# Working LayerNorms, last output products and gate by column halves, and router logits straight into token rows, in a four-layer decoder trunk

## The chip, the cores and the metric

The kernel runs on one core of a Trainium2 chip (NeuronCore, with TensorE, VectorE, ScalarE, GpSimd and SyncE). The metric is the device time of one execution, in microseconds (us).

## The reference, cut to what matters

256 tokens of 1024 float32 columns pass four layers. A layer has a token mixer (layers 0 and 3 a short convolution, layer 1 retention, layer 2 a spatial gate), a LayerNorm, a mixture of 16 experts, a second LayerNorm and a gated embedding:

```python
x = _layer_norm(ALPHA * x + mix, ln_g[i, 0], ln_b[i, 0])
ffn = _moe(x, router_w, router_b, moe_w_gate[i], moe_w_up[i], moe_w_down[i])
x = _layer_norm(ALPHA * x + ffn, ln_g[i, 1], ln_b[i, 1])
emb = p[i] @ ple_w_proj[i]
gate = jax.nn.sigmoid(x @ ple_w_gate[i] + ple_b_gate[i])
x = x + gate * emb
```

The router inside `_moe` takes `sigmoid(hf @ router_w)` (1024 x 16), picks a group of four experts and two experts in it for every token, and weights their outputs.

## The kernel before, in words

The tokens are two tiles of 128 rows, `t` = 0 and 1, held in `x[:, t, :]` (token rows by 1024 columns). Weights of mixer, embedding projection and gate come as slots of 1 MB (128 x 2048), numbered through all layers; `starts[L]` gives the slot number of layer L's mixer, of its projection (one slot) and of its gate (four slots). Precision is kept by splitting each operand in a high and a low part: ScalarE copies a slot to `w_hi`, VectorE writes `w_lo` (one 128x2048 subtraction, L1319), and `product` issues three fp32r matmuls. `split_behind(used)` on ScalarE and VectorE splits all slots below `used + 4`. The activations are turned by TensorE (`transpose_tile`, L523, eight transposes, two PSUM banks or "quads" of four), then ScalarE saves `xT_hi` and VectorE `xT_lo` (`save_tile`); `turned_tile` makes TensorE wait for both quads' low parts. `k` = 3L+1, 3L+2 and 3L+3 number the turned versions of x in a layer.

`rows_slot` multiplies one slot for one tile: j = 0, 1 (128 rows of contraction each) by c = 0, 1 (512-column halves, each its own PSUM bank). The last slot of tile 0 gives `done`; for tile 1 `weights_used` is the signal.

A LayerNorm of one tile on VectorE is: `residual` (two L1345), `layer_norm` with two `bn_stats` (L1383), aggregation, then `moments`, a chain of small instructions each waiting for the one before, beside which the two halves of (x - mean) * g run (L1391), then one 128x1024 instruction times rstd plus b (L1396), which increments `x_tile_ready`. TensorE's transposes of a tile wait for that.

`route` computes the logits transposed: the stationary operand is `rw_pad` (high part of the router weights in columns 0 to 15, low part in 16 to 31, zeros behind), the moving operand is `xT`, 16 matmuls of 128 columns per tile (L779). ScalarE copies the result to `logitsT`, and two matmuls with `fold` (L798) turn it back to token rows and add the parts. In layers 1 and 2 the logits of tile 0 stand ahead of the embedding products of tile 0, in layers 0 and 3 behind the transposes of tile 1. Behind the logits TensorE has the embedding products of tile 1, and only then the two rank matmuls that the choice of experts waits for (L806, L807).

The experts run as eight pairs, 12 slots of 1 MB each, loaded by SyncE's queue as places come free (96 per layer, an order and places from `expert_places`). All engines go through the pairs in a written order. At the end `put_back` adds the last pair's rows into PSUM banks 0 to 3 (L844), c = 0 for both tiles and then c = 1 for both, and `ffn_done` counts. Then VectorE splits the first gate slot (`split_behind(n_gate - 3)`), reads the flag `crowded` and skips the code for crowded experts, and begins the second LayerNorm: tile 0, `save_tile`, three more gate slots split, tile 1, `save_tile`. TensorE does gate slots 0 to 2 of tile 0, transposes tile 1, slot 3, then tile 1. The gate itself is, per tile, two additions of `bgate` (L1766), one sigmoid over 1024 columns on ScalarE, and two 128x1024 instructions on VectorE (L1771, L1772). When tile 1 of a gate is done GpSimd loads the next layer's `p_in` (L481) to `emb`, and TensorE's `turn_p` (L544) waits for that. The last gate is followed by two stores of 128x1024.

## Time and profile before

| | us |
|---|---|
| median of 3 runs | 1782.9 (1781.86 to 1783.79) |
| the profiled execution, its own time | 1777.66 |
| its span, first to last instruction | 1775.9 |
| TensorE busy | 1644.1 (93%) |
| VectorE busy | 717.1 (40%) |
| ScalarE busy | 468.7 (26%) |

The profile holds one execution. Engines are PE (TensorE matmul), PEld (its weight loads), DVE (VectorE), ACT (ScalarE), POOL (GpSimd), SP (SyncE). L12 is line 12 of the kernel. A group in a timeline merges neighbours of one kind; in square brackets stands how long the engine was idle before it and what released it.

### The profile page before, as it was taken

To read this page: it belongs to the slowest core of one execution; us is meant where nothing else is said; L and a number is where in the kernel's file an instruction comes from. 1 tells how busy PE (TensorE), PEld (TensorE's weight loads), DVE (VectorE), ACT (ScalarE), POOL (GpSimd) and SP (SyncE) were. 2 spreads that over 40 slices of the span, in tenths; PEclk is the share of its full clock that TensorE was granted. 3 is DMA by queue.
4 is the path that set the end of the run, shared out by engine and by line. 5 is a ranking of instruction groups with operands and counts; after the bars stand their busy time and mean duration, and the time that the engine had idled before them with its cause. 6 is when DMAs were issued, how large, how long until landed. Compare 5 with 4: busy or idle time off the path is not lost.

```text
span 1775.9 us, 17856 instructions
## 1 busy us (share of the span) xinstructions
PE 1644.1 (93%) x7564; PEld 988.0 (56%) x7564; DVE 717.1 (40%) x1030; ACT 468.7 (26%) x545; POOL 16.8 (1%) x34
## 2 busy tenths in 40 slices
PE   6989999869999899998799999899996998999976
PEld 5874443258777743433588777544334877434325
DVE  3572111174757621111856656311116666111125
ACT  4531111044443211111344333211102452111111
POOL 0000000000000000000000000000000000000000
PEclk9989999989999999999899999899998998999998
DMA  7488999945443899999565447999994557999990
GB/s 282 177 347 319 423 421 421 420 190 205 163 173 133 331 386 421 422 420 421 190 261 197 148 151 282 367 420 421 421 421 200 207 228 303 376 422 421 420 387 24
DMA packets 77180, 547.99 MB, mean 309 GB/s; under 512 B 8608, under 2 KB 8608, under 8 KB 12320
## 3 DMA queue, kind: packets, MB, share of 16 engines
q1 hardware_dynamic: 73296, 530.95, 74.1%
q0 software_dynamic: 3792, 15.73, 2.4%
q8 instruction: 68, 1.11, 0.2%
q14 instruction: 24, 0.20, 0.0%
HBM read 545.60 MB, written 1.05 MB: 308 GB/s over the span
## 4 chain that ended last, share of the span: by engine, by line
PE 75%; DVE 12%; DMA 8%; ACT 3%; issue 2%; SPq 0%; ACTq 0%; DVEq 0%
PE psum L834 33%; PE psum L512 10%; PE psum L514 10%; PE psum L513 10%; DMA expert_work<-in_experts 6%; PE psum L826 4%; DVE w_lo L1319 4%; PE psum L844 3%; PE psum L523 3%; ACT w_hi L1028 2%; PE psum L779 1%; DVE x L1391 1%; DVE x L1396 1%; DVE x L1345 1%; DMA raw<-in_slots 1%
## 5 line engine op out<-in xcount | busy, mean ns | idle before, releaser
L1319 DVE TENSOR_TENSOR w_lo<-raw,w_hi 128x2048 fp32r<-128x2048 f32 x120 | 271.2, 2288 | 169.2 <-ACT w_hi L1028 168.2
L512 PE MATMUL psum<-w_hi,xT_hi 128*128 128x512 f32 x704 | 283.8, 403 | 17.5 <-DVE w_lo L1319 11.1
L513 PE MATMUL psum<-w_lo,xT_hi 128*128 128x512 f32 x704 | 279.0, 396 | 0.0
L514 PE MATMUL psum<-w_hi,xT_lo 128*128 128x512 f32 x704 | 278.8, 396 | 0.0
L1028 ACT ACTIVATE w_hi<-raw 128x2048 fp32r<-128x2048 f32 x120 | 224.9, 1909 | 97.0 <-PE psum L514 88.3
L834 PE MATMUL psum<-raw,xg 128*64 128x512 f32 x896 | 211.9, 599 | 3.8 <-DMA raw<-in_experts 3.8
L1028 ACT ACTIVATE work<-psum 128x512 f32<-128x512 f32 x156 | 90.9, 593 | 431.0 <-PE psum L514 207.0
L1319 DVE TENSOR_TENSOR work_r<-psum,work_r 128x512 fp32r<-128x512 f32 x84 | 56.7, 689 | 363.2 <-ACT work_r L1028 363.2
L512 PEld LDWEIGHTS psum<-w_hi,xT_hi 128*128 128x128 f32 x704 | 135.8, 193 | 51.7 <-DVE xT_lo L1319 9.3
L514 PEld LDWEIGHTS psum<-w_hi,xT_lo 128*128 128x128 f32 x704 | 135.1, 192 | 29.1
L513 PEld LDWEIGHTS psum<-w_lo,xT_hi 128*128 128x128 f32 x704 | 135.5, 193 | 27.8 <-issue 0.2
L1028 ACT ACTIVATE work_r<-psum 128x512 fp32r<-128x512 f32 x84 | 48.5, 598 | 331.5 <-PE psum L834 330.4
L834 PE MATMUL psum<-expert_work,xg 128*64 128x512 f32 x552 | 129.0, 598 | 0.0
L834 PEld LDWEIGHTS psum<-raw,xg 128*64 128x64 f32 x896 | 59.2, 136 | 114.0 <-issue 99.4
L834 PE MATMUL psum<-expert_high,xg 128*64 128x512 f32 x472 | 113.1, 600 | 1.7 <-DMA expert_high<-in_experts 1.6
L512 PE MATMUL psum<-w_hi,work_r 128*128 128x512 f32 x224 | 90.0, 402 | 11.6 <-DVE work_r L1319 10.6
L1028 ACT ACTIVATE xg<-psum 128x512 f32<-128x512 f32 x64 | 38.2, 597 | 213.3 <-PE psum L826 213.3
L523 PE MATMUL psum<-const,x 128*128 128x128 f32 x192 | 32.9, 328 | 66.2 <-DVE x L1396 60.9
L514 PE MATMUL psum<-w_hi,work_r 128*128 128x512 f32 x224 | 88.3, 394 | 0.0
L513 PE MATMUL psum<-w_lo,work_r 128*128 128x512 f32 x224 | 88.1, 393 | 0.0
L834 PE MATMUL psum<-expert_work,work 128*64 128x512 f32 x344 | 80.0, 595 | 3.4 <-DMA expert_work<-in_experts 3.4
L826 PEld LDWEIGHTS psum<-work_r 128*128 128x128 f32 x512 | 65.7, 190 | 27.2 <-issue 22.7
(151 smaller groups left out, 1470.6 us busy)
## 6 DMA issues: line engine op xcount, KB each, us to landing
raw<-in_experts SPq DMA_DIRECT2D x148, 1024.0 KB, 15.6
raw<-in_slots SPq DMA_DIRECT2D x120, 1024.0 KB, 4.9
expert_work<-in_experts SPq DMA_DIRECT2D x112, 1024.0 KB, 14.9
expert_high<-in_experts SPq DMA_DIRECT2D x96, 1024.0 KB, 15.7
expert_norm<-in_experts SPq DMA_DIRECT2D x20, 1024.0 KB, 13.8
ln_par<-in_ln_g POOLq DMA_DIRECT2D x8, 512.0 KB, 8.1
ln_par<-in_ln_b POOLq DMA_DIRECT2D x8, 512.0 KB, 12.0
expert_y<-in_experts SPq DMA_DIRECT2D x4, 1024.0 KB, 15.1
```

The costliest lines, as they stand in the source:

```text
L512: mm(out, lhs[0], rhs[0], start=start, stop=False)
L513: mm(out, lhs[0], rhs[1], start=False, stop=False)
L514: return mm(out, lhs[1], rhs[0], start=False, stop=stop)
L523: last = nc.tensor.transpose(psum[:, bank, i * P:(i + 1) * P], c, ident[:, :])
L779: last = mm(psum[:, 4, t * P:(t + 1) * P], rw_pad[:, j, :], xT[i][:, j, t * P:(t + 1) * P], start=i == 0 and j == 0, stop=i == 1 and j == ...
L826: last = mm(psum[:, bank, j * SEQ:(j + 1) * SEQ], x_split[a][:, t, chunk], pick[:, t, Q * SEQ:(Q + 1) * SEQ], start=t + a == 0, stop=t + a ...
L834: last = mm(psum[columns(e), bank, :], lhs(j, e), w[:, 2 * j + e, :], start=start and j == 0, stop=stop and j == 1)
L844: last = mm(psum[:, bank0 + 2 * t + c, :], where[:, t * P:(t + 1) * P], what[i][:, c * NB:(c + 1) * NB], start=start and i == 0, stop=stop ...
L1028: return nc.scalar.activation(dst, src, func)
L1319: return tt(lo, whole, hi.bitcast(F), ALU.subtract)
L1345: step(stt(xs, xs, ALPHA, psum[:, bank0 + 2 * t + c, :], ALU.mult, ALU.add))
L1391: step(stt(x[:, t, cols], x[:, t, cols], nmv[:, 0, 0:1], ln_par[:, 0, cols], ALU.subtract, ALU.mult))
```

## The change

- The residual and the statistics of a LayerNorm are done half by half (`add_rows`). The half c = 0 starts when its own columns are ready: `rows_slot` runs the last slot c by c and signals `half_done` when c = 0 is complete, and `put_half` does so for the experts' rows of tile 0.
- The last instruction of a LayerNorm is two of 512 columns, with `x_half_ready` and `x_tile_ready`; each quad of transposes waits for its own half.
- In the second LayerNorm the first gate slot's `w_lo` moves from ahead of tile 0's LayerNorm to between it and `save_tile`.
- The gate products wait quad by quad (`turned_quad`). The gate's additions, sigmoid, product and sum, and the final stores, are halves.
- The logits go straight into token rows: `xT` is stationary, the router weights (16 columns, `rw_split`) move; 24 matmuls per tile (high x high, high x low, low x high). `rw_pad`, `fold`, `logitsT`, the copy and L798 go. For tile 1 the 16 matmuls on `xT_hi` come ahead of the wait for `xT_lo`.
- The load into the place `xg` waits for `logits_done`, which comes in place of the transposed logits' signal.

```diff
-                    sp.wait_ge(logitsT_in_psum, L + 1)
+                    sp.wait_ge(logits_done, L + 1)
...
-                sp.wait_ge(x_tile_ready, 2 * (3 * DEPTH - 1) + t + 1)
-                sp.dma_start(out[0, t * P:(t + 1) * P, :], x[:, t, :]).then_inc(s_out, 16)
+                for c, ready in enumerate((x_half_ready, x_tile_ready)):
+                    cols = slice(c * NB, (c + 1) * NB)
+                    sp.wait_ge(ready, 2 * (3 * DEPTH - 1) + t + 1)
+                    sp.dma_start(out[0, t * P:(t + 1) * P, cols], x[:, t, cols]).then_inc(s_out, 16)
...
             def transpose_tile(k, t):
-                if k == 0:
-                    pe.wait_ge(s_x[t], 16)
-                else:
-                    pe.wait_ge(x_tile_ready, 2 * (k - 1) + t + 1)
                 for q in range(2):
+                    if k == 0:
+                        pe.wait_ge(s_x[t], 16)
+                    else:
+                        pe.wait_ge((x_half_ready, x_tile_ready)[q], 2 * (k - 1) + t + 1)
...
+                order = [(j, c) for j in range(2) for c in range(2)]
+                if s == count - 1:
+                    order = [(j, c) for c in range(2) for j in range(2)]
+                for j, c in order:
+                    last = product(psum[:, 2 * t + c, :], part(lhs, ALL, 2 * s + j, t),
+                                   part(w, ALL, 2 * j + c), s == 0 and j == 0, s == count - 1 and j == 1)
+                    if s == count - 1 and (j, c) == (1, 0) and done is not emb_in_psum:
+                        last.then_inc(half_done, 1)
...
+                def logits(t, q, a, b, start=False, stop=False):
+
+                    for j in range(4 * q, 4 * q + 4):
+                        last = mm(psum[:, 4, t * NE:(t + 1) * NE], xT[a][:, j, t * P:(t + 1) * P], rw_split[b][:, j, :],
+                                  start=start and j == 4 * q, stop=stop and j == 4 * q + 3)
                     return last
 
+                def logits_of_first_tile():
+                    for q in range(2):
+                        turned_quad(k, 0, q)
+                        logits(0, q, 0, 0, start=q == 0)
+                        logits(0, q, 0, 1)
+                        logits(0, q, 1, 0, stop=q == 1)
...
-                logits(1).then_inc(logitsT_in_psum, 1)
-                pe.wait_ge(logitsT_ready, L + 1)
-                for t in range(T):
-                    last = mm(psum[:, 6, t * NE:(t + 1) * NE], logitsT[:, t * P:(t + 1) * P], fold[:, :],
-                              start=True, stop=True)
+                for q in range(2):
+                    pe.wait_ge(xt_hi, 4 * k + 2 + q + 1)
+                    logits(1, q, 0, 0, start=q == 0)
+                    logits(1, q, 0, 1)
+                for q in range(2):
+                    turned_quad(k, 1, q)
+                    last = logits(1, q, 1, 0, stop=q == 1)
...
-                for t in range(T):
-                    put_back(place[1], y, t, 0, False, True)
+                put_back(place[1], y, 0, 0, False, True).then_inc(put_half, 1)
+                put_back(place[1], y, 1, 0, False, True)
...
-                turned_tile(3 * L + 2, 0)
                 for i in range(4):
+                    if i % 2 == 0:
+                        turned_quad(3 * L + 2, 0, i // 2)
...
-            def residual(t, bank0):
-
-                for c in range(2):
-                    xs = x[:, t, c * NB:(c + 1) * NB]
-                    step(stt(xs, xs, ALPHA, psum[:, bank0 + 2 * t + c, :], ALU.mult, ALU.add))
+            def add_rows(t, c):
+
+                xs = x[:, t, c * NB:(c + 1) * NB]
+                link(stt(xs, xs, ALPHA, psum[:, 2 * t + c, :], ALU.mult, ALU.add))
+                step(nc.vector.bn_stats(stats[:, t, c, :], xs))
...
-                stt(x[:, t, :], x[:, t, :], rstd, ln_par[:, 1, :], ALU.mult, ALU.add
-                    ).then_inc(x_tile_ready, 1)
+                for c, ready in enumerate((x_half_ready, x_tile_ready)):
+                    cols = slice(c * NB, (c + 1) * NB)
+                    stt(x[:, t, cols], x[:, t, cols], rstd, ln_par[:, 1, cols], ALU.mult, ALU.add).then_inc(ready, 1)
...
-                split_behind(n_gate - 3)
+                dve.wait_ge(put_half, L + 1)
+                add_rows(0, 0)
...
                 dve.wait_ge(ffn_done, T * L + 1)
-                residual(0, 0)
+                add_rows(0, 1)
                 layer_norm(0, 2 * L + 1)
+                split_behind(n_gate - 3)
                 save_tile(3 * L + 2, 0)
                 split_behind(starts[L][2])
                 dve.wait_ge(ffn_done, T * L + 2)
-                residual(1, 0)
+                for c in range(2):
+                    add_rows(1, c)
                 layer_norm(1, 2 * L + 1)
...
-                    dve.wait_ge(ple_sig, 2 * L + t + 1)
-                    link(tt(ple[:, t, :], ple[:, t, :], emb[:, t, :], ALU.mult))
-                    tt(x[:, t, :], x[:, t, :], ple[:, t, :], ALU.add).then_inc(x_tile_ready, 1)
+                    for c, ready in enumerate((x_half_ready, x_tile_ready)):
+                        cols = slice(c * NB, (c + 1) * NB)
+                        dve.wait_ge(ple_sig, 4 * L + 2 * t + c + 1)
+                        link(tt(ple[:, t, cols], ple[:, t, cols], emb[:, t, cols], ALU.mult))
+                        tt(x[:, t, cols], x[:, t, cols], ple[:, t, cols], ALU.add).then_inc(ready, 1)
```

## Rows read from the trace of the kernel before

**Rows 1.** Busy time by stretch: PE, PEld, DVE, ACT, POOL; granted clock, DMA share, GB/s.

```profile
146.00:358.00 212.00, 207.22 (x975) 80.55 (x972) 30.93 (x55) 28.09 (x46) 1.05 (x2) 1.00 1.00 412
358.00:408.00 50.00, 36.59 (x156) 29.24 (x156) 41.78 (x54) 18.60 (x16) 2.49 (x5) 0.86 0.45 173
632.00:636.00 4.00, 4.00 (x20) 1.29 (x18) 0.00 (x0) 0.00 (x0) 0.00 (x0) 1.00 0.73 260
1370.00:1372.00 2.00, 2.00 (x6) 1.53 (x5) 0.96 (x2) 0.28 (x1) 0.00 (x0) 0.50 0.96 315
```

**Rows 2.** Waits: who waited for whom, us in total, times, longest.

```profile
PE psum L523 <- DVE x L1396: 60.9, 12, 9.0
```

**Rows 3.** Timeline of VectorE behind layer 0's experts: start, us, instruction.

```profile
358.31 2.29 DVE L1319 TENSOR_TENSOR w_lo<-raw,w_hi 128x2048 fp32r<-128x2048 f32 x1 [1.11 <-ACT w_hi L1028]
360.52 1.28 DVE L1345 SCALAR_TENSOR_TENSOR x<-x,psum 128x512 f32<-128x512 f32 x2
...
366.13 1.28 DVE L1396 SCALAR_TENSOR_TENSOR x<-x,nrstd,ln_par 128x1024 f32<-128x1024 f32 x1
...
370.71 6.68 DVE L1319 TENSOR_TENSOR w_lo<-raw,w_hi 128x2048 fp32r<-128x2048 f32 x3
377.31 1.28 DVE L1345 SCALAR_TENSOR_TENSOR x<-x,psum 128x512 f32<-128x512 f32 x2
...
382.92 1.28 DVE L1396 SCALAR_TENSOR_TENSOR x<-x,nrstd,ln_par 128x1024 f32<-128x1024 f32 x1
```

**Rows 4.** Timeline of TensorE in the same stretch.

```profile
357.25 1.20 PE L844 MATMUL psum<-work_r 128*128 128x512 f32 x4 [0.29 <-DVE work_r L1319]
367.47 1.97 PE L523 MATMUL psum<-const,x 128*128 128x128 f32 x8 [9.02 <-DVE x L1396]
370.85 0.79 PE L512 MATMUL psum<-w_hi,xT_hi 128*128 128x512 f32 x1 [1.41 <-DVE xT_lo L1319]
384.26 1.10 PE L523 MATMUL psum<-const,x 128*128 128x128 f32 x8 [2.72 <-DVE x L1396]
```

**Rows 5.** Instructions on x by form: ns min/median/max, first and last start.

```profile
L1345 DVE SCALAR_TENSOR_TENSOR x<-x,psum x32: 677/680/687, 108.5 to 1745.1; 128x512 f32<-128x512 f32 x32
...
L1391 DVE SCALAR_TENSOR_TENSOR x<-x,nmv,ln_par x32: 739/743/746, 111.3 to 1748.1; 128x512 f32<-128x512 f32 x32
```

**Rows 6.** Timeline of TensorE in layer 0's routing.

```profile
124.58 1.97 PE L523 MATMUL psum<-const,x 128*128 128x128 f32 x8 [3.85 <-DVE x L1396]
126.20 1.95 PE L779 MATMUL psum<-xT_hi,rw_pad 128*128 128x128 f32 x8
...
131.36 1.91 PE L779 MATMUL psum<-xT_lo,rw_pad 128*128 128x128 f32 x8
...
134.61 0.77 PE L512 MATMUL psum<-w_hi,emb_r 128*128 128x512 f32 x1
```

**Rows 7.** Timeline of TensorE in layer 1's routing.

```profile
604.68 1.00 PE L779 MATMUL psum<-xT_hi,rw_pad 128*128 128x128 f32 x8
...
611.95 1.09 PE L523 MATMUL psum<-const,x 128*128 128x128 f32 x8 [2.55 <-DVE x L1396]
614.61 1.97 PE L779 MATMUL psum<-xT_hi,rw_pad 128*128 128x128 f32 x8 [1.57 <-DVE xT_lo L1319]
...
619.63 0.77 PE L512 MATMUL psum<-w_hi,emb_r 128*128 128x512 f32 x1
```

**Rows 8.** Timeline of ScalarE in the same stretch.

```profile
610.40 1.06 ACT L1028 ACTIVATE work_r<-x 128x1024 fp32r<-128x1024 f32 x1
```

**Rows 9.** Timeline of VectorE at the last gate.

```profile
1767.75 1.42 DVE L1766 TENSOR_TENSOR work<-psum,bgate 128x512 f32<-128x512 f32 x2 [5.72 <-PE psum L514]
...
1771.60 1.22 DVE L1772 TENSOR_TENSOR x<-x,work 128x1024 f32<-128x1024 f32 x1
```

**Rows 10.** The chain that ended last, layer 0's gate: start, us, what.

```profile
406.56 3.13 DMA emb<-in_p
```

**Rows 11.** Timeline of ScalarE behind layer 0's experts.

```profile
356.37 3.70 ACT L1028 ACTIVATE w_hi<-raw 128x2048 fp32r<-128x2048 f32 x2
```

More of the change, by code:

```diff
@@ L198, in build @@
         conv_w = conv_w.rearrange("p (i w j) -> p i w j", i=2, w=3)
-        rw_pad = sb("rw_pad", KD, P, dt=FR)
-        fold = sb("fold", NE)
+        rw_split = [sb(f"rw_{part}", KD, NE, dt=FR)[:, :, :] for part in ("hi", "lo")]
         stats = sb("stats", T, 6, 6)
@@ L286, in build @@
         xt_in_psum, xt_ready = sem("xt_in_psum"), sem("xt_ready")
-        x_tile_ready = sem("x_tile_ready")
+        x_half_ready, x_tile_ready, half_done = sem("x_half_ready"), sem("x_tile_ready"), sem("half_done")
+        put_half = sem("put_half")
         mix_done, mix_read = sem("mix_done"), sem("mix_read")
@@ L595, in rows_slot @@
                 w = slot(n + s)
-                for j in range(2):
-                    for c in range(2):
-                        last = product(psum[:, 2 * t + c, :], part(lhs, ALL, 2 * s + j, t),
-                                       part(w, ALL, 2 * j + c), s == 0 and j == 0, s == count - 1 and j == 1)
+                order = [(j, c) for j in range(2) for c in range(2)]
[6 more added lines that the diff above has]
+                        last.then_inc(half_done, 1)
                 if t == 1:
@@ L1104, in conv_mixer @@
                     act.wait_ge(s_const, 16)
-                    act.wait_ge(rw_zeroed, 1)
-                    copy(rw_pad[:, :, 0:NE], rw[:, :, :]).then_inc(rw_hi_ready, 1)
+                    copy(rw_split[0], rw[:, :, :]).then_inc(rw_hi_ready, 1)
                 for k in range(4):
@@ L1200, in route @@
             def route(L):
-                act.wait_ge(logitsT_in_psum, L + 1)
-                copy(logitsT, psum[:, 4, 0:SEQ]).then_inc(logitsT_ready, 1)
                 act.wait_ge(logits_done, L + 1)
-                copy(score[:, :, :], psum[:, 6, 0:T * NE].rearrange("p (t e) -> p t e", t=T), ACT.Sigmoid
+                copy(score[:, :, :], psum[:, 4, 0:T * NE].rearrange("p (t e) -> p t e", t=T), ACT.Sigmoid
                      ).then_inc(score_ready, 1)
@@ L1292, in _ @@
                             save_tile(3 * L + 3, 0)
[L1293 to L1294 removed]
+                    for c in range(2):
+                        cols = slice(c * NB, (c + 1) * NB)
+                        act.wait_ge(ple_arg, 4 * L + 2 * t + c + 1)
+                        copy(ple[:, t, cols], ple[:, t, cols], ACT.Sigmoid).then_inc(ple_sig, 1)
         @block.vector
@@ L1378, in layer_norm @@
             def layer_norm(t, k, banks_read=None):
-                ready = steps[0]
-                for c in range(2):
-                    dve.wait_ge(dve_step, ready - 1 + c)
-                    step(nc.vector.bn_stats(stats[:, t, c, :], x[:, t, c * NB:(c + 1) * NB]))
                 dve.wait_ge(dve_step, steps[0])
@@ L1720, in experts @@
                                     xs = x[:, t, c * NB:(c + 1) * NB]
-                                    last = stt(xs, psum[:, 4 + 2 * t + c, :], 1 / ALPHA, xs, ALU.mult, ALU.add)
+                                    scale = 1 / ALPHA if t + c else 1.0
+                                    last = stt(xs, psum[:, 4 + 2 * t + c, :], scale, xs, ALU.mult, ALU.add)
                             last.then_inc(o["vector"], 1)
                     dve.wait_ge(o["vector"], len(OVER["vector"]) * PAIRS * ROUNDS)
+                    nc.vector.bn_stats(stats[:, 0, 0, :], x[:, 0, 0:NB]).then_inc(o["vector"], 1)
+                    dve.wait_ge(o["vector"], len(OVER["vector"]) * PAIRS * ROUNDS + 1)
             save_tile(0, 0)
@@ L1727, in _ @@
                 (conv_mixer, retention_mixer, sgu_mixer)[L % 3](L)
-                end = starts[L][1]
+                end, n_gate = starts[L][1:3]
                 split_behind(end - 4)
+                dve.wait_ge(half_done, 4 * L + 1)
+                add_rows(0, 0)
                 wait_rows(dve, L, 0, mix_done, L + 1, end)
-                residual(0, 0)
+                add_rows(0, 1)
                 layer_norm(0, 2 * L)
@@ L1748, in _ @@
                 dve.wait_ge(ffn_done, T * L + 1)
-                residual(0, 0)
+                add_rows(0, 1)
                 layer_norm(0, 2 * L + 1)
+                split_behind(n_gate - 3)
                 save_tile(3 * L + 2, 0)
@@ L1753, in _ @@
                 dve.wait_ge(ffn_done, T * L + 2)
-                residual(1, 0)
+                for c in range(2):
+                    add_rows(1, c)
                 layer_norm(1, 2 * L + 1)
                 save_tile(3 * L + 2, 1)
-                n_gate = starts[L][2]
                 dve.wait_ge(bg_loaded, 16 * (L + 1))
```

46 lines of the change are left out of this document (19 added, 27 removed).

## The prediction

> **What bounds the kernel now.** I read the page first: a span of 1775.9 us (the table above). Then the busy time by stretch [rows 1]: during layer 0's experts PE is busy 207.22 of 212 us at the full clock with DMA at 1.00, so two resources are full and nothing the change touches is. From the end of the experts through the gate PE works 36.59 of 50 us while DVE works 41.78: here LayerNorm on DVE sets the pace. The waits [rows 2] say the same: transposes waited 60.9 us, 12 times, for the last instruction of a LayerNorm. So I followed DVE and PE in order of time behind the experts [rows 3, 4], in routing [rows 6 to 8], and at the end [rows 9].
>
> The reader is to see in [rows 3, 4]: the last expert rows are issued at 357.25 (TensorE's L844); DVE then splits a gate slot (358.31 to 360.60), and only then starts the residual (360.52); 5.61 us later (366.13) starts the last instruction, 1.28 us. PE has been idle 9.02 us when it transposes, and 1.41 us more before its first product at 370.85. Tile 1 repeats it: three slots split from 370.71, residual at 377.31, transposes at 384.26 after 2.72 us idle. Behind these PE is full again, so what tile 1's transposes gain passes on.
>
> **Second LayerNorm and gate, four times.** (a) w_lo moved: 2.29 us leave the path ahead of tile 0's LayerNorm. (b) Tile 0's half c = 0 is added behind the last y rows (357.2) and costs 0.68 + 0.04 + 0.68 = 1.40 us [rows 5], the statistics taking as long, so to 358.6, while TensorE ends c = 1. The second half then starts at 358.6 and gives its statistics at 360.05; before, residual and statistics took 2.5 us from 360.52. Gain (a) and (b): 2.97 us; the last instruction starts at 363.16. (c) As two halves it costs 2 x 0.743 less 0.07 overlap = 1.41 for 1.28 us, but quad 0 can be transposed 0.55 us earlier than before the split. That helps little for tile 0: the moved w_lo now stands between, 364.55 to 366.8, and xT_lo of quad 0 follows at 367.45. The first product starts at 367.5 for 370.85, 3.3 us earlier. (d) The three w_lo start at 368.0 and end at 374.6; tile 1's four half steps, each waiting for the one before, take 2.75 for 2.51 us, the last instruction starts at 380.5, x_half is ready at 381.25 and x_tile at 381.9. Quad 1 is turned by 382.5, when slot 3 begins; before, 385.1. **2.6 us per layer, 10.4 in all.** What PE gained in tile 0 is lost again in a longer wait for tile 1. SP's queue has no part: the gate slots were issued from 335.77 on, the first row of the queue behind the experts, and landed before their splits.
>
> **The gate's halves** gain nothing between layers: PE goes on with tile 1's slots. They cost: product and sum as four linked halves take about 2.76 for 2.49 us, the projection's input is loaded after that, and TensorE waits for its landing [rows 10]: +0.25, three times, **+0.8**. Behind the last gate nothing covers them: from 1767.75 to 1772.82 [rows 9] 5.07 us; now half 0 is added while half 1 is multiplied by TensorE, then come 0.73 of addition and 2.8 of halves: 3.55. The last store is half as large. **-1.8.**
>
> **Routing.** The new logits are 24 matmuls per tile of 16 moving columns. Their nearest price is the old one, which has the same 128x128 fp32r loads: from 126.20 to 131.36, 24 matmuls, 0.215 us each at 1.2 GHz [rows 6], about 0.105 at 2.4 GHz (the eight at 604.68, [rows 7]). I take these, since the stationary load was already what spaced 128 moving columns.
> Layers 0 and 3: the halves bring transposes 1.1 us forward (0.55 by the statistics of half 0, 0.55 by the split; DVE is held by a w_lo until 116.9). From there 48 matmuls instead of 32 (+3.4 us), no copy and no fold (133.07 to 134.61, -1.5). Together **+0.8 each**.
> Layers 1 and 2: tile 0's logits stand in the shadow of tile 1's LayerNorm (8 more, 0.85 us warm; PE idled 2.55 there). For tile 1 the LayerNorm ends 1.0 us earlier, but ScalarE, whose split of x at 610.40 moves behind the later embedding copy to 611.25, frees xT_hi only at 612.85, when 24 matmuls start: 612.9 + 5.1 = 618.0 for 619.63 [rows 7, 8]. **-1.6 each.** The load into `xg` then waits for a signal that comes at the same time as its old one.
> Routing in all: 1.6 - 3.2 = **-1.6**. Is it passed through the experts? DMA fills up only behind their first products, so an earlier start moves the whole stretch as long as DMA has idle time to give; in the tightest, layer 1, DMA had 27% of 4 us free at 632 [rows 1], 1.1 us, and smaller gaps after it. I count it all.
>
> **Unseen terms.** The `crowded` test on DVE (read a flag, skip code) was under the 2.29 us w_lo, which left no gap [rows 3], so it costs at most 2.2 us; now only 0.68 us of statistics cover it. Between 0 and 1.5 us is exposed, four times (0 to 6 us). ScalarE does the same between two copies of 1.85 us that stand back to back [rows 11], so I stay low: +0.3 each, **+1.2**. The clock: behind tile 1's transposes it was at 0.50 in layer 2 (1370 to 1372, six matmuls started in 2 us, [rows 1]) but at 1.00 in layer 0, after PE had stood idle. The new idle, 378.2 to 381.3 and between quads, is some 0.7 us longer. A cold stretch of 3.5 us costs half of itself, 1.8 us; four layers, two of them cold already: 0 to +3.8, I take **+1.0**.
>
> The Trainium skill (Runtime: NRT & Kernel Launch, Instruction fetch mechanics) says that a taken branch out of the two fetched pages waits for a DMA fetch, which speaks against moving cover off this skip; the row only shows that the wait, if any, is under 2.2 us. At that bound the sum would be 4.8 us worse.
>
> **Sum**: -10.4 + 0.8 - 1.8 - 1.6 + 1.2 + 1.0 = -10.8 us. The profiled execution's own 1777.66 (1.76 outside the span) would become 1766.9; the median of runs lies 5.2 above it, so I predict 1782.9 - 10.8 = **1772.1 us**.
>
> **Rivals.**
> 1. Skip exposed: DVE stands 1.5 us before tile 0's second half in each layer. For: nothing else covers it. Against: ScalarE's gapless row. +4.8: 1777. Chance 0.11.
> 2. Clock lost: longer gaps and 2.5 us of light 16-column matmuls let the clock fall also in layers 0 and 1's gate and before the embedding products of layers 1 and 2; 2.8 more in the gate, 1.2 x 2 in routing: 1777. For: it fell in layers 2 and 3. Against: in layer 1 the transposes at 611.95 were still warm behind 2.55 us of idle [rows 7]. Chance 0.12.
> 3. Both, or one with the experts giving nothing back: 1780 to 1783, no measurable change. Chance 0.05.
> 4. Cheap loads: not the load but the 128 moving columns bound L779, and 16 columns are spaced by half, 0.107 at 1.2 GHz. Layers 0 and 3 gain 5.1 each, layers 1 and 2 (held by xT_lo until 614.2) 2.9 each: 1756. Against: with 128 columns the spacing is twice the array time, so the load binds. Chance 0.06. The Trainium skill (TensorE: Matmul & The Clock Gate, LDWEIGHTS) puts a load at columns / 1.2 ns, 107 ns for 128; no row shows that for this type at 1.2 GHz.
> 5. Slower: a 16-column matmul costs two passes, as a plain f32 one (L798, two instructions each, 0.43 us) does. Then routing pays 48 x 0.215 in layers 0 and 3 (10.3 each) and 5.1 + 2 in layers 1 and 2: +35 in all, 1807. It decides from about 0.29 us per matmul: 144 of them on the path (2 x 48 + 2 x 24) x 0.075 = 10.8. Against: operands stay fp32r, one instruction each in L779. Chance 0.03.
> The forecast itself: 0.63.
>
> **How the numbers follow.** Faster by over 0.2% (3.6 us, about what can be told from no change) is the forecast, 1, 2 and 4: 0.92; same 0.05; slower 0.03. The range takes in 1 and 2 with a margin for a skip and clock in between, to 1778, and below a warm routing in layers 1 and 2 (3 us) and no exposed terms (2.2), with 1 more: 1765. Outside lie 3, 4, 5 and small tails, under 0.2.
>
> **What the new profile would show.** Right: from the last expert row to the residual's second half about 1.3 us; transposes at 6.7 us behind it for 10.2; idle before tile 1's transposes above 3 us; first gate product 3.3 us earlier; logits 0.21 us apart at 1.2 GHz; score about 0.8 later against the mixer's end in layers 0 and 3, 1.5 earlier in 1 and 2. Wrong: a gap on DVE behind `put_half` with nothing running; cold matmuls in slot 3 of layers 0 and 1; logits at another spacing; a layer whose experts end no earlier though they start earlier.

## The result: faster, by 17 to 21 us where 10.8 were predicted

Changed kernel: 1761.15 us (median of 4 runs, 1759.79 to 1763.59), beside 1782.38 for the kernel before (4 runs). The ratio is 0.9884, 95% interval 0.9859 to 0.9909, so 16 to 25 us less. Two more sets of runs of the same kernel, with the experiments, gave 0.9905 (0.9881 to 0.9929) and 0.9890 (0.9871 to 0.9909). The predicted 1772.1 us is a ratio of 0.9939: right in direction, too small, and 1765, the lower end of the range, is above the measured time. The profiled spans are 1775.9 and 1758.2 us, 17.7 less, with a mean granted clock of 0.965 and 0.970.

The page of the changed kernel:

```profile
span 1758.2 us, 17988 instructions
...
PE 1650.8 (94%) x7612; PEld 993.7 (57%) x7612; DVE 721.3 (41%) x1060; ACT 468.7 (27%) x549; POOL 16.8 (1%) x34
```

Busy time by stretch, columns as in [rows 1]:

```profile
146.00:358.00 212.00, 206.48 (x971) 79.88 (x968) 31.19 (x56) 27.24 (x45) 1.05 (x2) 1.00 1.00 411
358.00:408.00 50.00, 39.80 (x172) 31.57 (x172) 43.01 (x61) 20.52 (x20) 3.36 (x6) 0.86 0.49 186
846.00:863.00 17.00, 11.70 (x45) 9.12 (x44) 16.58 (x24) 4.79 (x4) 0.00 (x0) 0.80 0.08 32
863.00:875.00 12.00, 12.00 (x52) 10.10 (x51) 7.86 (x10) 5.84 (x6) 1.81 (x3) 0.89 0.53 177
```

PE's share is 94% for 93, DVE's 41% for 40. The experts' stretch is as full as before. In the 50 us from 358 PE now gets 39.80 us done for 36.59, since the stretch holds more products. DVE is as busy as it was: it is still what sets the pace here, only with less ahead of it.

VectorE behind layer 0's experts, as [rows 3]:

```profile
357.66 0.68 DVE L1356 SCALAR_TENSOR_TENSOR x<-x,psum 128x512 f32<-128x512 f32 x1
358.37 0.69 DVE L1357 BATCH_NORM_STATS2 stats<-x 128x6 f32<-128x512 f32 x1
359.52 0.69 DVE L1356 SCALAR_TENSOR_TENSOR x<-x,psum 128x512 f32<-128x512 f32 x1 [0.45 <-PE psum L855]
...
364.07 1.41 DVE L1406 SCALAR_TENSOR_TENSOR x<-x,nrstd,ln_par 128x512 f32<-128x512 f32 x2
365.40 2.29 DVE L1331 TENSOR_TENSOR w_lo<-raw,w_hi 128x2048 fp32r<-128x2048 f32 x1
...
368.80 6.68 DVE L1331 TENSOR_TENSOR w_lo<-raw,w_hi 128x2048 fp32r<-128x2048 f32 x3
375.40 0.68 DVE L1356 SCALAR_TENSOR_TENSOR x<-x,psum 128x512 f32<-128x512 f32 x1
...
381.26 1.41 DVE L1406 SCALAR_TENSOR_TENSOR x<-x,nrstd,ln_par 128x512 f32<-128x512 f32 x2
383.39 1.35 DVE L1331 TENSOR_TENSOR xT_lo<-psum,xT_hi 128x512 fp32r<-128x512 f32 x2 [0.72 <-ACT xT_hi L1041]
```

TensorE there, as [rows 4]:

```profile
357.80 1.20 PE L855 MATMUL psum<-work_r 128*128 128x512 f32 x4 [0.29 <-DVE work_r L1331]
364.87 1.97 PE L522 MATMUL psum<-const,x 128*128 128x128 f32 x8 [5.87 <-DVE x L1406]
368.34 0.79 PE L511 MATMUL psum<-w_hi,xT_hi 128*128 128x512 f32 x1 [1.50 <-DVE xT_lo L1331]
...
382.07 1.32 PE L522 MATMUL psum<-const,x 128*128 128x128 f32 x8 [2.50 <-DVE x L1406]
383.14 0.47 PE L511 MATMUL psum<-w_hi,xT_hi 128*128 128x512 f32 x1
```

Counted from the last expert row (357.25 before, 357.80 now), tile 0's transposes come after 7.07 us for 10.22, its first product after 10.5 for 13.6, tile 1's transposes after 24.27 for 27.01. The first half of the residual starts before the last row is issued; the gap ahead of the second half, where the flag is read and code skipped, is 0.45 us here (0.18, 0.52 and 0.17 in layers 1 to 3).

Layer 1's routing, TensorE, as [rows 7]:

```profile
602.51 0.51 PE L786 MATMUL psum<-rw_hi,xT_hi 128*128 128x16 f32 x4
602.87 0.59 PE L786 MATMUL psum<-rw_lo,xT_hi 128*128 128x16 f32 x4
...
604.65 0.59 PE L786 MATMUL psum<-rw_hi,xT_lo 128*128 128x16 f32 x4
...
609.35 1.24 PE L522 MATMUL psum<-const,x 128*128 128x128 f32 x8
612.15 0.61 PE L786 MATMUL psum<-rw_hi,xT_hi 128*128 128x16 f32 x4 [1.57 <-ACT xT_hi L1041]
...
614.69 1.85 PE L786 MATMUL psum<-rw_hi,xT_lo 128*128 128x16 f32 x8
616.40 0.77 PE L511 MATMUL psum<-w_hi,emb_r 128*128 128x512 f32 x1
```

Granted clock behind tile 0's logits there, 1.00 in the 2 us before:

```profile
606.00:610.00 4.00, 4.00 (x15) 3.12 (x14) 2.50 (x9) 0.42 (x1) 0.00 (x0) 0.57 1.01 428
```

Logits with 16 moving columns start 0.111 us apart at the full clock (16 from 602.87 to 604.65) and 0.214 at half (eight from 614.69 to 616.40). Layer 2 came out differently:

```profile
1105.97 1.32 PE L522 MATMUL psum<-const,x 128*128 128x128 f32 x8
1108.52 0.61 PE L786 MATMUL psum<-rw_hi,xT_hi 128*128 128x16 f32 x4 [1.23 <-ACT xT_hi L1041]
...
1110.33 1.04 PE L786 MATMUL psum<-rw_hi,xT_lo 128*128 128x16 f32 x8
```

All 24 logits of tile 1 run at the full clock here, and the next product starts 5.25 us after the transposes began; with the old logits it was 7.69 there.

The last gate, VectorE, as [rows 9]:

```profile
1752.48 0.69 DVE L1784 TENSOR_TENSOR work<-psum,bgate 128x512 f32<-128x512 f32 x1 [0.67 <-PE psum L513]
...
1755.13 0.69 DVE L1791 TENSOR_TENSOR x<-x,work 128x512 f32<-128x512 f32 x1
```

From the bias addition behind the last product (now one half, before two) to the end of the span it is now 5.7 us, for 8.15.

Where the 17.7 us of the two profiled executions lie, by layer 0 to 3 (us, time after less time before):

| stretch | 0 | 1 | 2 | 3 | sum | predicted |
|---|---|---|---|---|---|---|
| up to the first gather of the experts | -0.4 | -1.8 | -3.9 | +1.6 | -4.6 | -1.6 |
| experts | +1.0 | +1.0 | 0.0 | -1.4 | +0.6 | 0 |
| last expert row to tile 1's transposes | -2.7 | -3.0 | -2.7 | -3.0 | -11.4 | -10.8 |
| from there to the next layer's first embedding transposes, or the end | 0.0 | +1.4 | -0.1 | -3.7 | -2.3 | +1.6 |

(Predicted, third row: four times 3.0 earlier, less 1.2 for the skip, is -10.8. Fourth row: of the 3.0 only 2.6 were to pass slot 3 of tile 0, four times +0.4, and +1.6 + 0.8 + 1.0 - 1.8 = +1.6. The first row counts from the embedding transposes, in layer 0 from the start of the span; what stands there ahead of the mixer's end took 0.3 us longer.)

### The profile page after: what moved, and what is told of

Its sections match the earlier page's. It is cut to its first block, busy times and chain, and to the rows that moved or that the text cites. A ratio compares the mean times of both kernels' runs of the same rounds, so it can differ in the third digit from the quotient of the medians.

```text
span 1758.2 us, 17988 instructions
## 1 busy us (share of the span) xinstructions
PE 1650.8 (94%) x7612; PEld 993.7 (57%) x7612; DVE 721.3 (41%) x1060; ACT 468.7 (27%) x549; POOL 16.8 (1%) x34
## 4 chain that ended last, share of the span: by engine, by line
PE 76%; DVE 12%; DMA 8%; ACT 2%; issue 1%; SPq 0%; DVEq 0%; ACTq 0%
PE psum L845 34%; PE psum L511 10%; PE psum L512 10%; PE psum L513 10%; DMA expert_work<-in_experts 6%; DVE w_lo L1331 4%; PE psum L837 4%; PE psum L855 3%; PE psum L522 2%; PE psum L786 2%; ACT w_hi L1041 1%; DVE work_r L1331 1%; DMA raw<-in_slots 1%; DVE x L1399 1%; DVE stats L1357 1%
## 5 line engine op out<-in xcount | busy, mean ns | idle before, releaser
L1663 DVE TENSOR_REDUCE cg<-psum 128x1 f32<-128x256 f32 x32 | 13.6, 425 | 160.2 <-PE psum L899 160.2
## 6 DMA issues: line engine op xcount, KB each, us to landing
ln_par<-in_ln_b POOLq DMA_DIRECT2D x8, 512.0 KB, 11.4
```

## The experiments

Each set is timed beside the kernel before on its own chip. Their medians of before were 1780.62 (21 runs: `again`, `wlo_only`, `wlo_back`, `route_only`), 1783.14 (15 runs: `warm`, `route_back`, `gate_full`, `before_again`) and 1781.32 (9 runs: the last four), so ratios are compared, not times.

| run | median (n), us | ratio to before, 95% |
|---|---|---|
| again | 1763.67 (6) | 0.9905 (0.9881 to 0.9929) |
| wlo_only | 1770.57 (6) | 0.9940 (0.9920 to 0.9960) |
| wlo_back | 1773.77 (10) | 0.9961 (0.9945 to 0.9978) |
| route_only | 1779.61 (12) | 0.9996 (0.9979 to 1.0013) |
| route_back | 1764.22 (5) | 0.9898 (0.9876 to 0.9921) |
| gate_full | 1763.56 (6) | 0.9892 (0.9866 to 0.9917) |
| warm | 1773.08 (10) | 0.9954 (0.9937 to 0.9970) |
| before_again | 1779.65 (1) | single run |
| third | 1764.51 (5) | 0.9890 (0.9871 to 0.9909) |
| warm_fit | 1763.70 (5) | 0.9897 (0.9882 to 0.9913) |
| lo_late | 1762.52 (5) | 0.9888 (0.9873 to 0.9904) |
| late_t1 | 1752.09 (5) | 0.9830 (0.9814 to 0.9847) |

**again**, the changed kernel as it is.

> The changed kernel once more. Chain theory (the time comes out of LayerNorm's and the gate's chain as worked out before, and the clock only adds chance): the gain against before varies between executions with where the clock falls, 17 to 21 us in the median, and the stretches ruled by VectorE (last expert row to tile 1's transposes) repeat to 0.5 us at 24.0 us, while those in which TensorE ran cold differ by 1 to 3 us between this profile and the first one. Rival (all of the excess is a fixed mis-sizing): every stretch repeats within 0.3 us.

Measured -17 us for -21; the two intervals overlap, and the gain stays above 10.8 (12.6 at the least). As the chain theory had it, the stretches from the last expert row to tile 1's transposes repeat within 0.02 us, and those in which TensorE's clock fell differ by up to 1.8.

**wlo_only**: the kernel before with the w_lo alone moved.

```diff
-                split_behind(n_gate - 3)
...
                 layer_norm(0, 2 * L + 1)
+                split_behind(starts[L][2] - 3)
                 save_tile(3 * L + 2, 0)
```

> The kernel before with one edit: the first gate slot's w_lo moves behind tile 0's second LayerNorm. Chain theory: VectorE had 1.84 + 0.16 us idle waiting for xT_hi, which the moved 2.29 us now fill, so tile 1's transposes come 2.0 us earlier behind the last expert row in each layer, 8 us in all: ratio 0.9955. Clock theory (most of the gain of the whole change is TensorE running at the full clock in stretches where it was cold): under 4 us from the chain, and the rest follows the cold time in the profile, up or down.

10 us less: the move alone does half or more of what the change does. Tile 1's transposes come 24.53 to 24.55 us after the last row in every layer, 2.47 sooner. VectorE of this kernel:

```profile
359.32 1.28 DVE L1345 SCALAR_TENSOR_TENSOR x<-x,psum 128x512 f32<-128x512 f32 x2 [0.83 <-PE psum L844]
...
366.14 2.28 DVE L1319 TENSOR_TENSOR w_lo<-raw,w_hi 128x2048 fp32r<-128x2048 f32 x1
```

Where the w_lo stood there is a gap of 0.83 us and then the residual. Before, the 2.29 us were not all: VectorE had first waited 1.11 us for ScalarE's w_hi [rows 3]. My step (a) priced the move at the instruction's duration. The times of step (b) left the wait out all the same, so the sum of both did not suffer.

**wlo_back**: the changed kernel with the w_lo put back ahead of tile 0's first half.

```diff
+                split_behind(n_gate - 3)
                 dve.wait_ge(put_half, L + 1)
...
                 layer_norm(0, 2 * L + 1)
-                split_behind(n_gate - 3)
```

> The changed kernel with the first gate slot's w_lo put back ahead of tile 0's LayerNorm (ahead of the early half). Chain theory: 2.0 us slower than the changed kernel per layer, 8 us, so about 12 to 13 us faster than before. If the clock gives most of the gain, the loss is under 4 us.

Half to two thirds of the gain is gone. Its VectorE:

```profile
358.79 2.29 DVE L1331 TENSOR_TENSOR w_lo<-raw,w_hi 128x2048 fp32r<-128x2048 f32 x1 [1.11 <-ACT w_hi L1041]
361.00 0.68 DVE L1356 SCALAR_TENSOR_TENSOR x<-x,psum 128x512 f32<-128x512 f32 x1
...
362.86 0.69 DVE L1356 SCALAR_TENSOR_TENSOR x<-x,psum 128x512 f32<-128x512 f32 x1 [0.45 <-issue]
```

The wait of 1.11 us is back, and tile 1's transposes are 26.7 to 27.1 us behind the last row, as in the kernel before: with the w_lo ahead of them the halves bring 0.3 us at most in this LayerNorm. There is a gap of 0.45 us which here no other engine ends ("issue"; 0.17, 0.52 and 0.17 in layers 1 to 3), so this is the price of the flag and the skip on VectorE itself. It is rival 1's mechanism, at 1.3 us over four layers for my 1.2 and its 6.0.

**route_only**: the kernel before with the new logits alone. **route_back**: the changed kernel with the old ones (padded weights, copy, fold).

```diff
-                            last = mm(psum[:, 4, t * P:(t + 1) * P], rw_pad[:, j, :],
-                                      xT[i][:, j, t * P:(t + 1) * P], ...
+                        last = mm(psum[:, 4, t * NE:(t + 1) * NE], xT[a][:, j, t * P:(t + 1) * P], rw_split[b][:, j, :],
```

> The kernel before with the new logits alone. Chain theory: layers 0 and 3 lose 1.9 us each (48 matmuls at 0.215 for 32, without copy and fold), layers 1 and 2 gain 1.2 each if the clock is as before: +1.4 us, no measurable change. Clock theory: the logits of 16 moving columns change where the clock falls; with it held in layers 1 or 2 the time is 3 to 5 us below before, with it falling ahead of the embedding products 2 to 3 us above.

> The changed kernel with the old transposed logits, copy and fold. Chain theory with the prices of the first profile: layers 0 and 3 take about 10.0 instead of 11.4 us from tile 1's transposes to the end of the logits, layers 1 and 2 7.7 instead of 5.3 to 7.1: -2.8 + 3.0, so within 2 us of the changed kernel if the clock is as it was there. Clock theory: layer 1 does not fall ahead of its embedding products (cold from 606.3 in the changed kernel), and the time moves by 1 to 3 us with the cold stretches.

Neither direction can be told from nothing. The traces say why: from the end of the mixer (tile 0's transposes) to the experts' first gather the new logits take 1.3 us more than the old in layer 0, 2.2 more in layer 3, 0.3 less in layer 1 and 3.2 less in layer 2 (the changed kernel against `route_back`), 0.1 in sum. In layer 2 the changed kernel keeps the full clock from the transposes through the last logit, where the old way does not. Which layer keeps it is no property of the layer: in `route_only` it is layer 1 that gains (20.98 us in this stretch for 25.41 in the kernel before) and layer 2 that does not (24.14 for 24.60).

**gate_full**: the changed kernel with the gate's sigmoid, product and sum and the last stores at full width.

```diff
-                    for c, ready in enumerate((x_half_ready, x_tile_ready)):
-                        cols = slice(c * NB, (c + 1) * NB)
-                        dve.wait_ge(ple_sig, 4 * L + 2 * t + c + 1)
-                        link(tt(ple[:, t, cols], ple[:, t, cols], emb[:, t, cols], ALU.mult))
-                        tt(x[:, t, cols], x[:, t, cols], ple[:, t, cols], ALU.add).then_inc(ready, 1)
+                    dve.wait_ge(ple_sig, 2 * L + t + 1)
+                    link(tt(ple[:, t, :], ple[:, t, :], emb[:, t, :], ALU.mult))
+                    tt(x[:, t, :], x[:, t, :], ple[:, t, :], ALU.add).then_inc(x_tile_ready, 1)
```

> The changed kernel with the gate's sigmoid, product, sum and the stores over 1024 columns again (the additions of bgate stay halves). Chain theory: 2.4 us lost behind the last gate, 0.25 gained three times at the projection's input: 1.7 us slower than the changed kernel. Rival (the halves gave part of the missing gain inside the layers too): 4 us or more.

Its time is not distinguishable either, as terms of +0.8 and -1.8 have to be. Its trace shows both terms. From the last bias addition to the end it takes 7.4 us for the 5.7 of the halves, and between layers the embedding transposes start 0.87 us behind tile 0's last transposes for 1.11 to 1.17. Its routing code is that of the changed kernel, but layer 1 kept its clock (0.57 in the changed kernel's stretch above):

```profile
606.00:610.00 4.00, 4.00 (x23) 3.13 (x22) 3.54 (x13) 0.00 (x0) 0.00 (x0) 1.00 1.01 426
610.05 1.32 PE L520 MATMUL psum<-const,x 128*128 128x128 f32 x8
```

Tile 1's transposes come 9.31 us behind tile 0's there, for 10.48 in the changed kernel, and the first gather 20.60 for 23.63: the same instructions, 3.0 us apart, and the clock is what differs.

**before_again**: one more execution of the kernel before.

> The kernel before once more, one look. If the first profile of before was a lucky draw of the clock, the stretches from the last expert rows to tile 1's transposes are 27.0 us again, while those behind tile 1's transposes and in routing come out 1 to 2 us longer in some layers, and the span lies nearer the median of its runs, 1779 us. Rival (the runs differ for another cause, DMA): the experts' stretches differ instead, by more than 1 us.

The span was 1777.9 us at a clock of 0.964, 2 us more than the profiled one. Tile 1's transposes are 27.0 us behind the last row again; the stretch behind them is 1.4 us longer in layer 0 and 1.5 shorter in layer 3, and from the mixer's end to the first gather it is 0.9 shorter in layer 0 and 1.2 longer in layer 3. A difference of this size in one layer of one pair of profiles is therefore no measure of a term. The profile that the sum was made against (1777.66) lies 3.0 to 5.5 us under the medians of before, the changed kernel's (1760.07) 1.1 to 4.4 under its own. So the profiles' 17.7 is as good an estimate of the gain as the medians' 17 to 21, and both are far from 10.8.

**warm**: idle time of TensorE filled with matmuls that nothing reads, 24 behind the last rows, 20 ahead of tile 1's transposes, 10 in routing of layers 0 and 3.

```diff
+                for _ in range(10 if L % 3 == 0 else 0):
+                    mm(psum[:, 7, :], pT[0][:, 0, 0:P], w_hi[:, starts[L][1] % HIGH, 0:NB], start=True, stop=True)
                 transpose_tile(k, 1)
...
+                def fill(n):
+                    for _ in range(n):
+                        mm(psum[:, 7, :], place[1][:, 0:P], y[0][:, 0:NB], start=True, stop=True)
+
+                fill(24)
                 transpose_tile(3 * L + 2, 0)
...
                     if i == 3:
+                        fill(20)
                         transpose_tile(3 * L + 2, 1)
```

> The changed kernel with matmuls of 512 columns whose result nobody reads, in TensorE's idle time: 24 behind the last expert rows, 20 ahead of tile 1's gate transposes, 10 ahead of tile 1's transposes in the routing of layers 0 and 3. Clock theory: the gate's stretches run at 2.4 GHz, tile 1's transposes stay where VectorE puts them (24.0 us behind the last rows), and from there to the next layer's input transposes 25.4 us instead of up to 27.3: 1.3 to 1.9 us in each of the layers that were cold; the routing gains up to 1.5 us in layers 0 and 3 before the light logits let the clock fall. 5 to 9 us faster than the changed kernel. Rival (the clock is not what differs): no change, or slower where a filler is still running when a half becomes ready.

The clock did rise, to 0.980, and the kernel became 9 to 12 us slower than the changed one (by the ratios). TensorE of `warm`:

```profile
356.78 1.20 PE L857 MATMUL psum<-work_r 128*128 128x512 f32 x4 [0.29 <-DVE work_r L1339]
362.99 7.46 PE L1025 MATMUL psum<-work_r 128*128 128x512 f32 x24 [5.01 <-issue]
370.28 1.04 PE L522 MATMUL psum<-const,x 128*128 128x128 f32 x8
```

The fillers wait for nothing, and yet the first starts 5.01 us behind the last row, "issue" (4.97, 5.08 and 4.03 in layers 1 to 3): between the two stands only the test that skips the guarded code of the experts. TensorE had read the flag long before, behind its first gathers (`pe.value_load`, ahead of the first pair), so reading it is no part of this gap. In the gap of layer 0, from 358 to 363, lies one transfer of 16 KB of the queue for instructions, as in the gaps of the other layers:

```profile
q8 instruction: 1, 0.02, 1.4%
```

So code is loaded in the gap; how much of the 5 us waits for it, the trace does not say. In the changed kernel the skip lies under the 5.87 us for which the transposes wait for x anyway. The 24 fillers started late, ended late, and held tile 0's transposes back until 370.28 where x had been ready at about 364; the 20 did the same to tile 1. From the last row to tile 1's transposes it is 5.0 to 6.1 us longer in each layer, 21.7 in all.

Elsewhere the fillers paid. In routing they filled the idle time ahead of tile 1's transposes, which came on time, and more than half of layer 0's logits ran at the full clock:

```profile
123.46 2.43 PE L802 MATMUL psum<-w_hi,emb_r 128*128 128x512 f32 x10
126.50 1.32 PE L522 MATMUL psum<-const,x 128*128 128x128 f32 x8 [0.62 <-DVE x L1414]
127.77 0.61 PE L786 MATMUL psum<-rw_hi,xT_hi 128*128 128x16 f32 x4
```

From the mixer's end to the first gather layer 0 took 20.96 us for 24.20 in the changed kernel, and layer 3 took 22.57 for 25.37: about 3 us each. Behind tile 1's gate transposes layers 1 and 2 took 25.6 us for 26.8 and 27.0. The clock theory was right there, and the loss behind the experts hid it. **warm_fit** asks if the overrun is the whole harm, with 5 and 10 fillers and none in routing.

> Changed kernel with 5 filler matmuls behind the last experts' rows and 10 ahead of the transposes of tile 1 (24, 20 and 10 in routing before). In the trace with 24 the first filler, which waits for nothing, began 4.97 to 5.01 us after the last row: that is what TensorE takes to get past the guarded experts, and the 24 then ended 5.4 us behind the row that they had to be ready for; 20 more held tile 1's transposes back. Theory (fillers were slow because they overran; TensorE's way past the guard costs nothing as long as the LayerNorm of 5.9 us covers it): no overrun now, so at most 0.3 us late per layer, the products of tile 0's gate are behind the transposes at a higher clock or not, and either way the LayerNorm of tile 1 on VectorE ends no sooner: ratio within 0.002 of the changed kernel beside it, granted clock 0.970 to 0.976. Rival (any filler harms, by power or by the write to the bank): slower by 4 us or more. Rival (a cold clock was on the path of the gate): 4 us faster or more.

0.9897 beside 0.9890 for the unchanged one (`third`, below), clock 0.974: no harm and no help that could be told. The five did overrun a little (tile 0's transposes came 0.9 to 1.4 us late, tile 1's 0.2 to 0.7), and behind the ten TensorE idled 2.93 us again ahead of tile 1's transposes, and its clock fell to half behind them in layers 0 and 1. So this run does not test what a clock held there is worth. The mean clock is no measure of the time: by 2 x (1 - clock) x span, 106 us at half clock became 71 in `warm` and 92 in `warm_fit`, and neither time fell. Where VectorE sets when tile 1 can go on, a faster TensorE gains nothing; it gains where its own matmuls are the path, as in routing.

**third** and **lo_late**. The second moves the last of the three w_lo from ahead of tile 1's LayerNorm to behind it.

```diff
-                split_behind(starts[L][2])
+                split_behind(n_gate - 1)
                 dve.wait_ge(ffn_done, T * L + 2)
                 for c in range(2):
                     add_rows(1, c)
                 layer_norm(1, 2 * L + 1)
+                split_behind(starts[L][2])
```

> The changed kernel once more, as it is, on the same chip as the three beside it. It gives the spread from run to run, without which differences of 0.2% between these kernels can't be read. By every theory a ratio of 0.989 to 0.991 to the kernel before.

> Changed kernel with the last of the three w_lo that stand ahead of tile 1's second LayerNorm moved behind it. Theory (VectorE's chain sets tile 1's transposes, 382.07): they come 2.3 us sooner, at 379.8; the fourth slot of tile 0 waits for its w_lo until 382.6 and begins there, not at 383.14; what follows comes 0.5 us sooner, 2.2 us in all. So of the 2.3 us only a quarter arrives, since the same subtraction now stands ahead of the products that need it. Rival (the whole 2.3 us arrive, 9 us in all): then the wait for the LayerNorm and not the products behind it was the path. Rival (no gain): xT_lo of tile 1, now behind the w_lo, comes later than the end of the fourth slot.

Not distinguishable from `third`. Tile 1's transposes do come 2.2 us sooner in each layer, and in the profiled execution (the longest of its five, 1769.34 us) it is all lost behind them:

```profile
380.64 1.32 PE L522 MATMUL psum<-const,x 128*128 128x128 f32 x8 [1.68 <-DVE x L1406]
383.50 0.79 PE L511 MATMUL psum<-w_hi,xT_hi 128*128 128x512 f32 x1 [1.54 <-DVE w_lo L1331]
384.10 0.63 PE L512 MATMUL psum<-w_lo,xT_hi 128*128 128x512 f32 x1
384.52 0.63 PE L513 MATMUL psum<-w_hi,xT_lo 128*128 128x512 f32 x1
```

Slot 3 of tile 0 now waits 1.54 us for its own w_lo, and after two idle times in a row its products start 0.42 to 0.43 us apart, at half the clock; at 0.23 apart they would have ended 2.3 us sooner.

**late_t1**: all four slots of tile 0, then tile 1's transposes.

```diff
-                    if i == 3:
-                        transpose_tile(3 * L + 2, 1)
                     rows_slot(starts[L][2], 4, tiled(xv), 0, 0, i, ple_done)
+                transpose_tile(3 * L + 2, 1)
```

> Changed kernel with tile 1's transposes of the gate put behind all four slots of tile 0 and not ahead of the fourth. Now TensorE idles 2.50 us behind the third slot (379.18 to 382.07) while VectorE ends tile 1's LayerNorm, then runs the fourth slot (12 products, 2.7 us) under the copies of the transposes. Theory (this idle time is what is left of the LayerNorm on the path): the fourth slot fills the idle time and ends at about 382, the transposes run 382.1 to 383.1, and the first product of tile 1 waits for xT_hi and xT_lo until about 385.0 where it now starts at 385.9: 0.9 us less per layer, 3.5 us in all, ratio 0.002 below the changed kernel beside it. Rival (VectorE's chain behind, with tile 0's gate rows and the copies in another order, sets the end): no change. Rival (the copies take as long as the fourth slot did, 2.7 us and more): up to 1 us slower per layer.

The best kernel of the case, 12 us below `third` on the same chip and 29 below the kernel before; the mechanism holds, the expected 3.5 us were too few.

```profile
380.53 0.39 PE L513 MATMUL psum<-w_hi,xT_lo 128*128 128x512 f32 x1
381.83 1.32 PE L522 MATMUL psum<-const,x 128*128 128x128 f32 x8 [0.91 <-DVE x L1405]
383.91 0.50 PE L511 MATMUL psum<-w_hi,xT_hi 128*128 128x512 f32 x1 [0.76 <-DVE xT_lo L1330]
```

TensorE idles 0.91 us ahead of the transposes and 0.76 behind them, for 2.50 and nothing: I had the copies take 1.9 us. Tile 1's first product starts 2.08 us after its transposes, where in the changed kernel 12 more products lie between, to 385.99, and it is 3.92: 1.8 us per layer for my 0.9. The rest of the 9.4 us below is in layers 1 and 2, where the changed kernel lost clock and this one did not. Compare the stretch behind tile 1's transposes with 863 to 875 above (0.89):

```profile
843.00:860.00 17.00, 15.34 (x57) 11.97 (x58) 15.87 (x25) 4.83 (x5) 1.05 (x2) 0.81 0.05 14
860.00:872.00 12.00, 11.81 (x56) 9.47 (x55) 10.06 (x12) 7.95 (x7) 0.76 (x1) 1.00 0.92 346
```

From tile 1's transposes to the next layer's embedding transposes it takes 23.8 to 24.0 us in layers 0 to 2 for the changed kernel's 25.5, 26.8 and 27.0. The two kernels' spans differ by 10.1 us, of which 9.4 lie in this stretch and its like at the end.

## Why the prediction was right and wrong

**Right: the step from the last rows to tile 1's transposes.** x_half was predicted at 381.25 for transposes at 384.26 before, 3.0 us sooner, and 0.3 given back to the skip. Measured: 2.7 to 3.0 sooner. `wlo_only` and `wlo_back` divide it otherwise than I had: moving the w_lo is worth 2.47 and not 2.29, because ScalarE's wait goes with it, and the halves add 0.2 to 0.6, once it is gone.

**Right: the spacing of the logits**, 0.214 us at half and 0.111 at the full clock; rivals 4 (0.107 at half clock) and 5 (0.43) are out. The Trainium skill (TensorE: Matmul & The Clock Gate, LDWEIGHTS) puts a load of 128 columns at 107 ns; for this type the rows give 0.214 us at 1.2 GHz, with 16 moving columns as with 128, and the measurement decides. Layers 0 and 3 were predicted +0.8 each. From the mixer's end it is -0.7 and +1.6, and +0.2 and +0.4 against `before_again`.

**Right: the skip**, 0.17 to 0.52 us per layer on VectorE, 1.3 in all for my 1.2. The Trainium skill (Runtime: NRT & Kernel Launch, Instruction fetch mechanics) has a taken branch out of the fetched pages wait for a load of code. A stall at the skipped code does show in this case, 4.0 to 5.1 us on TensorE and 0.17 to 0.52 on VectorE. On TensorE the flag was read some 200 us before and a load of code of 16 KB lies in the gap, which agrees with the page; on VectorE the read stands in the gap too, and no run here divides it from the skip. The profile named neither until something stood behind the skip that waited for nothing.

**Wrong, the routing term** of -1.6, for -4.6 in the profile. 2.3 of the missing 3.0 us are layer 2, -3.9 for -1.6: I priced its logits at half clock, from layer 1's [rows 7], and they ran at the full one. From the mixer's end on, `route_back` divides the term: the halves brought 5.0 us over the four layers (2.0, 1.5, 0.8 and 0.6 against the kernel before) where about 4.2 were in my sum (1.1 and 1.0, twice each), and the new logits cost 0.1 where 2.6 were in it, nearly all of that difference in layer 2.

Layer 1 met its number (-1.8 for -1.6) by luck. There the light matmuls did what rival 2 said: the embedding products of tile 0 ran at half clock behind them (0.57 from 606 to 610). This was not under cover of tile 1's LayerNorm. Its halves were ready from 608.1 us on (VectorE's last instructions start at 607.37), but the transposes start at 609.35, directly behind the last product. With its clock kept, as in `gate_full`, the layer takes 3.0 us less. The step that failed is that one clock was taken for all layers: the sum had logits at half clock, and the runs have them at either.

**Wrong, the clock term and the passing on** of the gate. I gave back 0.4 us per layer (3.0 to 2.6) for tile 0's slot 3, 0.8 for the halves and 1.0 for the clock, 3.4 in all, behind tile 1's transposes. In layers 0 and 2, where both kernels ran there at like clock, slot 3 and the halves should have cost 0.65 each and the stretch changed by 0.0 and -0.1. Layer 1 lost its clock, +1.4. In layer 3 the stretch to the end was 3.7 us shorter. Of these, 2.4 lie at the very end (5.7 for 8.15, [rows 9]), where I had 1.8: VectorE's instructions brought 1.7 for 1.5, and the time behind the last of them, with the smaller store, 0.7 for 0.3. The other 1.3 lie among the products before it, where the kernel before had lost clock behind tile 1's transposes and the changed one did not. So here the clock gave back in one layer what it took in another, where I had +1.0. Which layers fall to half clock behind the gap varies from run to run (layer 0 in `again`, layer 3 in `again` and `third`, neither in the profiled one), at 1.6 to 1.8 us each. That is 3.3 of the 4.9 us by which the span of `again` is longer, but only 1.3 of the 6.1 of `third`, where the start of the kernel and the experts differ more; it can be part of the difference between 17 and 21.

**Left open.** Experts differed by -1.4 to +1.0 us per layer, and by as much between two traces of the same kernel (215.1 and 216.7 in layer 0), so what they gave back of an earlier start can't be read by layer. In sum they took 862.5 and 863.4 us in the two profiles of the kernel before and 863.2, 863.4 and 865.3 in the three of the changed one, so most of the earlier start was passed on, as assumed. `gate_full` and the routing runs bound their terms to some 4 us each and no closer. The profiles' 17.7 leave -1 to 3.5 us of the medians' gain unexplained, within the spread of both kernels.

**The step that failed, in short.** The chain up to tile 1's transposes held (-11.4 us for -10.8). What failed is the price of TensorE's clock and of what stands behind the transposes: routing came out at -4.6 for -1.6, and the stretch behind tile 1's transposes at -2.3 for +1.6. No new mechanism put the result outside the range. The terms that I set on the slow side (skip, clock, passing on, halves, 4.6 us in all) had a range of 0 to +10 and none below nothing; but the clock can also be given back, and routing likewise. That the terms' errors all pointed one way is in part chance: with layer 1's clock kept too, the time would have been lower still.

## What to carry to other kernels

An instruction moved off the path takes the wait ahead of it along: read "start of the one before" to "start of the next", not its duration. When a LayerNorm holds TensorE up, first look for products that are ready and stand behind the transposes in program order: putting one slot ahead of them was worth 12 us, more than the halves and the routing together. Fill idle time with such work first. Matmuls that only keep the clock up pay where TensorE's own matmuls are the path behind them and they end before their successor is ready (`warm`, routing of layers 0 and 3, some 3 us each); behind the experts, where they overran, they cost 5 to 6 us per layer, and the mean clock rose all the same. No run here has them in routing alone. And where the clock falls in one run and not in the next, give its term a range on both sides of nothing.

## What the runs showed of the hardware

- TensorE needs 4.0 to 5.1 us to get past the guarded code behind the experts, the flag long read (eight gaps in `warm` and `warm_fit`); VectorE 0.17 to 0.52 us with the read (`wlo_back`). No row of the kernel before could show it, since both were covered.
- Matmuls of 16 columns with a 128x128 fp32r load each start 0.111 us apart at full clock, near the 0.105 of those with 128 columns [rows 7], and 0.214 at half clock. The loads of stationary operands are then busy without a gap (4.00 of 4.00 us from 127.5 to 131.5 in layer 0), so the load is the price and not the columns.
- Ahead of tile 1's gate transposes TensorE idled in every layer of the changed kernel. Behind 2.50 and 2.68 us of idle time (layers 0 and 3) the granted clock stayed at 1.00, behind 3.81 and 3.58 (layers 1 and 2) it fell to half. In `late_t1` the idle time was 0.9 us and less, and the clock stayed full behind it in all four layers.
- The same routing instructions of layer 1 took 23.63 us where its clock fell (the changed kernel) and 20.60 where it was kept longer (`gate_full`).
